# Four operand buffers with tiles 548 instead of 544 elements apart, in a two-layer hybrid encoder step

## What is computed

```python
def trunk(x, ...):
    for i in range(2):
        h = rmsnorm(x, norm_mix[i])
        if i % 2 == 0:
            u, v, z, xbc, dt_raw = split(h @ l0_w_in)
            ya, gm_v = gmlp_mix(u, v, ...)              # spatial gating in chunks of 128
            yb, ... = mamba_mix(z, xbc, dt_raw, ...)    # conv, state-space scan, norm
            x = x + concatenate([ya, yb]) @ l0_w_out
        else:
            x = x + retention_mix(h, ...)               # 8 heads, w_in 1024 x 6144, w_out 2048 x 1024
        h = rmsnorm(x, norm_ffn[i])
        x = x + (silu(causal_dwconv(h @ w_gate)) * (h @ w_up)) @ w_down      # d_ff 2816
        gate = sigmoid(rmsnorm(x, norm_ple[i]) @ ple_w_gate[i])
        x = x + gate * (p[i] @ ple_w_proj[i])
    return rmsnorm(x, norm_final), ...
```

## Time and profile before

| | |
|---|---|
| median of 3 runs | 1999.78 us (1998.51 to 2000.27) |
| span of the profiled execution | 1997.0 us |
| TensorE matmul busy | 1869.7 us, 94% |
| TensorE weight load busy | 1802.0 us, 90% |
| DVE, ACT, POOL busy | 48%, 31%, 44% |
| matmuls | 14,129, of which 12,864 at L310 |
| mean granted TensorE clock | 0.955 of full speed |

### The profile page before, as it was taken

The page is one execution under the profiler, slowest core; times in us unless marked ns, Lnnn a source line. Parts: engine busy times, 40 slices in busy tenths (PEclk is TensorE's granted clock), DMA queues, the critical chain, the costliest instruction groups (busy, mean ns, idle before and its releaser), DMA issues.

```text
span 1997.0 us, 34512 instructions
## 1 busy us (share of the span) xinstructions
PE 1869.7 (94%) x14129; PEld 1802.0 (90%) x14129; DVE 951.5 (48%) x1509; ACT 614.9 (31%) x886; POOL 877.9 (44%) x428
## 2 busy tenths in 40 slices
PE   3996997999999999999989999999989999999996
PEld 2995895789899999999989999999879999999995
DVE  1214585654755255155664444154445534524555
ACT  3241122223432222223443333233323422322342
POOL 4433142323754455456653333333335444544562
PEclk7995696999999999999999999999989999999998
DMA  4230020112123422222322222222212222222221
GB/s 141 85 105 26 23 85 9 43 43 74 64 85 109 135 85 95 96 77 71 106 75 82 82 71 72 94 75 83 72 42 80 93 87 85 95 96 82 71 92 45
DMA packets 49106, 156.23 MB, mean 78 GB/s; under 512 B 5969, under 2 KB 9937, under 8 KB 49010
## 3 DMA queue, kind: packets, MB, share of 16 engines
q1 hardware_dynamic: 43920, 146.75, 22.5%
q10 hardware_dynamic: 5090, 8.13, 1.2%
HBM read 149.23 MB, written 5.63 MB: 78 GB/s over the span
## 4 chain that ended last, share of the span: by engine, by line
PE 83%; DVE 9%; issue 3%; POOL 2%; ACT 2%; DMA 0%; DVEq 0%; SPq 0%; POOLq 0%; ACTq 0%
PE proj L310 73%; PE Q L891 8%; DVE arena L1361 1%; DVE op_lo L380 1%; DVE arena L1582 1%; ACT arena L601 1%; POOL ssq L396 1%; POOL arena L526 1%; DVE arena L1278 1%; PE Q L1111 0%; ACT op_hi L367 0%; DVE rstd L360 0%; POOL w_lo L405 0%; DVE x L1584 0%; DVE arena L1470 0%
## 5 line engine op out<-in xcount | busy, mean ns | idle before, releaser
L405 POOL TENSOR_TENSOR w_lo<-w_raw,w_hi 128x1024 fp32r<-128x1024 f32 (+2 forms) x276 | 654.8, 2373 | 817.3 <-ACT w_hi L331 817.0
L310 PE MATMUL proj<-op_hi,w_hi 128*128 128x256 f32 x4288 | 900.0, 291 | 43.6 <-POOL w_lo L405 20.6
L310 PE MATMUL proj<-op_hi,w_lo 128*128 128x256 f32 x4288 | 890.5, 289 | 0.0
L310 PE MATMUL proj<-op_lo,w_hi 128*128 128x256 f32 x4288 | 883.3, 287 | 0.0
L310 PEld LDWEIGHTS proj<-op_hi,w_hi 128*128 128x128 f32 x4288 | 689.2, 189 | 56.4 <-POOL w_lo L405 20.6
L310 PEld LDWEIGHTS proj<-op_lo,w_hi 128*128 128x128 f32 x4288 | 692.5, 189 | 0.0
L310 PEld LDWEIGHTS proj<-op_hi,w_lo 128*128 128x128 f32 x4288 | 688.0, 189 | 0.0
L331 ACT ACTIVATE w_hi<-w_raw 128x1024 fp32r<-128x1024 f32 (+2 forms) x276 | 284.7, 1032 | 710.1 <-PE proj L310 710.0
L1278 DVE TENSOR_TENSOR arena<-proj,rstd 128x512 f32<-128x512 f32 x153 | 105.6, 690 | 273.6 <-PE proj L310 273.0
L1285 DVE TENSOR_TENSOR x<-proj,x 128x512 f32<-128x512 f32 x72 | 49.8, 691 | 261.4 <-PE proj L310 261.4
L891 PE MATMUL Q<-arena 128*128 128x256 f32 (+9 forms) x604 | 140.4, 374 | 23.8 <-POOL arena L526 17.7
(11 more groups left out here) (149 smaller groups left out, 1003.0 us busy)
## 6 DMA issues: line engine op xcount, KB each, us to landing
w_raw<-in_w_gu SPq DMA_DIRECT2D x88, 512.0 KB, 3.3
w_raw<-in_w_down SPq DMA_DIRECT2D x32, 512.0 KB, 3.3
w_raw<-in_w_heads_a SPq DMA_DIRECT2D x30, 512.0 KB, 3.3
w_raw<-in_w_heads_b SPq DMA_DIRECT2D x18, 512.0 KB, 3.2
w_raw<-in_w_gate SPq DMA_DIRECT2D x16, 512.0 KB, 3.3
w_raw<-in_w_xbc SPq DMA_DIRECT2D x12, 512.0 KB, 3.4
w_raw<-in_w_down SPq DMA_DIRECT2D x16, 384.0 KB, 3.0
w_raw<-in_w_v SPq DMA_DIRECT2D x8, 512.0 KB, 4.9
```

Of the source, the lines that this page charges most:

```text
L310: last = nc.tensor.matmul(proj[:, 2 * g.mod(2) + half, 0:size], w[:, lo:lo + P], o[:, at:at + size], start=(k == 0 and j == 0), stop=(k == ...
L405: nc.gpsimd.tensor_tensor(w_lo[:, c:c + width], w_raw[:, c:c + width], w_hi[:, c:c + width], ALU.subtract).then_inc(w_lo_done, 1)
```

## The change

The pitch of the tiles in the four operand buffers becomes OP = T + 4 = 548 elements, so each buffer grows by 32 elements (128 bytes). The four elements behind each tile are never written or read. All reads and writes of the operand buffers use the new pitch. The arena is cut by 84 elements to make room. x and everything else keeps its pitch of 544. Tiles 6 and 7, which were written and read as one run of 1088 elements for p, become two runs of 544 with a gap between them (`two_ops`).

```diff
+OP = T + 4
@@
-        op_hi = [sb(f"op{i}_hi", KD * T, R) for i in range(2)]
-        op_lo = [sb(f"op{i}_lo", KD * T, R) for i in range(2)]
+        op_hi = [sb(f"op{i}_hi", KD * OP, R) for i in range(2)]
+        op_lo = [sb(f"op{i}_lo", KD * OP, R) for i in range(2)]
...
-        ARENA = 15200
+        ARENA = 15116
...
+        def two_ops(buf):
+            return buf[:, 6 * OP:8 * OP].rearrange("p (a b) -> p a b", a=2)[:, :, 0:T]
+
...
-                            at = (k0 + k) * T + half * HALF
+                            at = (k0 + k) * OP + half * HALF
...
-            nc.scalar.activation(part(op_hi[ops], n, 0, T), src, ACT.Copy, scale=col(gain, n))\
+            nc.scalar.activation(part(op_hi[ops], n, 0, T, OP), src, ACT.Copy, scale=col(gain, n))\
...
-            nc.vector.scalar_tensor_tensor(out=part(op_lo[ops], n, 0, T), in0=src, scalar=col(gain, n),
-                                           in1=part(op_hi[ops], n, 0, T), op0=ALU.mult, op1=ALU.subtract)\
+            nc.vector.scalar_tensor_tensor(out=part(op_lo[ops], n, 0, T, OP), in0=src, scalar=col(gain, n),
+                                           in1=part(op_hi[ops], n, 0, T, OP), op0=ALU.mult, op1=ALU.subtract)\
...
-                        run(op_hi[HID[layer]][:, 6 * T:8 * T], p_raw, ACT.Copy, "p_hi")
+                        run(two_ops(op_hi[HID[layer]]), two(p_raw), ACT.Copy, "p_hi")
...
-                        at = k * T + half * HALF
+                        at = k * OP + half * HALF
...
-                            tt(part(op_lo[HID[layer]], n.div(2), 0, T), h, part(op_hi[HID[layer]], n.div(2), 0, T), sub)\
+                            tt(part(op_lo[HID[layer]], n.div(2), 0, T, OP), h, part(op_hi[HID[layer]], n.div(2), 0, T, OP), sub)\
...
-                        tt(op_lo[HID[layer]][:, 6 * T:8 * T], p_raw, op_hi[HID[layer]][:, 6 * T:8 * T], sub)\
+                        tt(two_ops(op_lo[HID[layer]]), two(p_raw), two_ops(op_hi[HID[layer]]), sub)\
```

More of the change, by code:

```diff
@@ L676, in _ @@
                 act.wait_ge(sem("gm_ya"), 2 * g + 2)
-                run(part(op_hi[1], g, 0, T), ya[:, (g % 2) * T:(g % 2 + 1) * T], ACT.Copy, "gm_hi")
+                run(part(op_hi[1], g, 0, T, OP), ya[:, (g % 2) * T:(g % 2 + 1) * T], ACT.Copy, "gm_hi")
             act.dma_start(s_sample, A["ssm_state"]).then_inc(sem("s_in_loaded"), 16)
@@ L785, in turn5 @@
                             act.wait_ge(sem("r_mix"), (h * 4 + (2 * e + 3)).v)
-                            run(part(op_hi[1], tile + e, 0, T), sq[:, e * T:(e + 1) * T],
+                            run(part(op_hi[1], tile + e, 0, T, OP), sq[:, e * T:(e + 1) * T],
                                 ACT.Copy, "r_mhi")
@@ L849, in gate_up @@
                             act.wait_ge(tile_read, (n + (gu.g0 + 1)).v)
-                            run(part(op_hi[HID[layer]], n.div(2), 0, T), hid[:, q * T:(q + 1) * T], ACT.Copy,
+                            run(part(op_hi[HID[layer]], n.div(2), 0, T, OP), hid[:, q * T:(q + 1) * T], ACT.Copy,
                                 "f_hi")
@@ L1224, in turn5 @@
                     dve.wait_ge(sem("r_mhi"), (h * 2 + (e + 1)).v)
-                    tt(part(op_lo[1], tile + e, 0, T), sq[:, e * T:(e + 1) * T], part(op_hi[1], tile + e, 0, T), sub)\
+                    tt(part(op_lo[1], tile + e, 0, T, OP), sq[:, e * T:(e + 1) * T], part(op_hi[1], tile + e, 0, T, OP), sub)\
                         .then_inc(sem("r_mlo"), 1)
@@ L1323, in ya_low @@
                 dve.wait_ge(sem("gm_hi"), g + 1)
-                tt(part(op_lo[1], g, 0, T), ya[:, (g % 2) * T:(g % 2 + 1) * T], part(op_hi[1], g, 0, T), sub)\
+                tt(part(op_lo[1], g, 0, T, OP), ya[:, (g % 2) * T:(g % 2 + 1) * T], part(op_hi[1], g, 0, T, OP), sub)\
                     .then_inc(sem("gm_lo"), 1)
```

## The result

The kernel before takes 1999.18 us (median of 15 runs, 1997.98 to 2000.45), the changed one 2004.7 us (15 runs, 2002.61 to 2005.77). The ratio is 1.0026, with a 95% interval of 1.0018 to 1.0034: slower by 0.26%, some 5.5 us. The two sets of runs do not overlap, so the difference is real, small as it is.

The account below looks back on a forecast made before the run. The prediction took TensorE's matmul pace, 124.7 ns a matmul on L310, to bound the kernel. Its four parts summed to 0 on a median of 1999.8 us, giving 2000.0 us, with a range of 1982 to 2022 us.

Parts of the forecast that it names:

- the forecast's own case: Whole kernel: time stays the same, within about 0.2% (4 us) of no change; chance 0.64.
- Rival A: Moving reads inside a block take one block more: 64-byte blocks 65 us slower, chance 0.07; 32-byte 21.5 us, 0.12.
- Rival B: Starts equal modulo 128 collide, so the change helps: large 110 us faster, chance 0.05; small 17 us, 0.09.
- What bounds the kernel: TensorE has work for 94% of the span; the matmul line L310 is 73% of the chain of waits.
- Part 1: Copies on ACT, subtractions on DVE: no added instructions; second runs cost at most 0.22 and 0.27 us, on the path 0.
- Part 2: DVE and ACT writes into the operand buffers: 0 from starts off 64-byte boundaries, upper bound 4 us, no gain.
- C: Writes into the operand buffers cost their upper bound, the matmul pace unchanged: 2004 us, counted within the forecast's 0.64.
- Part 3: Matmuls' moving reads from the operand buffers: 9684 come to start off a 64-byte multiple, at 0 cost or gain.
- Part 4: Everything behind the operand buffers moves by 512 bytes, with the same residues modulo 512: 0.
- What would show it: Signs if right: 48 gate-phase pairs in 11.97 us, 0.748 us a tile in gu01, L380's minimum at 783 ns.

Follow-up runs that it names:

- the control: Changed kernel's buffer sizes and arena, but pitch 544 as before, so only what lies behind the buffers moves by 512 bytes; 1999.82 us in one run (before: 1999.15).

## Why the prediction was right or wrong, point by point

The forecast was 2000.0 us, "same". It came out 4.7 us above that, inside the range of 1982 to 2022, and slower by 0.26% where the forecast's own case ended at 0.2%. That the time lies in the range is in part luck: the range was spanned by rivals A and B, neither of which happened, and no term of the sum or rival has the mechanism that did. The effect was small enough to fit.

*What bounds the kernel* held. The only thing that moved was TensorE's pace, and it moved the span one to one (5.4 us of busy time, 5.3 us of span).

*Part 1, instructions: 0.* Right: 34,512 before and after, and the two copies of 1088 elements cost the same in two runs as in one (1099 and 1292 ns). The bounds of 0.22 and 0.27 us for a second run were far too wide.

*Part 2, writes: 0, at most 4 us.* Right at 0. C gives nearly the right time, 2004 us, for a reason that didn't occur: the writes kept their durations and the wait on them became shorter. A time that fits doesn't prove the mechanism.

*Part 3, moving reads: 0.* **This is the term that failed.** It measures +20 and +26 ns a slab of 48 matmuls, 0.47 ns a matmul. Over 12,864 matmuls that is 6.0 us at most, of which 5.3 show. The argument was that "every row in which an address varies gives 0". The rows compared tiles of before alone. They differ in the rhythm by up to 20 ns a tile, which I put down to the stream. All of these tiles have the same distance to their weights modulo 128 bytes, so the rows held the one quantity fixed that the change moves. I also asked only for the address of the moving operand, and set the weights aside since 16 columns of them go at the same pace as 128. That row says that the *amount* of weights doesn't matter; the run in which only the weights were moved, +67 ns a slab, says that their *place* does. The sentence on 16-byte cachelines (the Trainium skill, page "SBUF — State Buffer", section "Door 1: The DMA port swizzle") counted as many lines at either pitch, and by it the sum stayed 0. The measured pace differs among layouts with equal counts of such lines, from 5.947 to 6.080 us a slab, so the rule doesn't price this.

*Part 4, the shift by 512 bytes: 0.* Right, shown by the control.

*Rival A* had the sign, not the mechanism. Tile 0, aligned to 64 bytes, takes 0.76 us and tile 3, 48 bytes off, 0.74. The kernel in which nothing is aligned runs at before's pace. And A's prices of 21.5 and 65 us are 4 and 12 times what was found.

*Rival B* (equal starts collide, the change helps) is refuted for this change: the tiles no longer start alike modulo 128 and are slower. Its idea that the rhythm of 0.74 and 0.75 us holds something to be gained has a grain of truth: half of the phases at +16 bytes take 5.947 us. The others take 6.053, and the kernel as a whole is 3.5 us slower.

*What would show it.* The 11.97 us of the gate phase was the right place to look. But its 0.06 us is only six times the 0.01 us to which a start is read, the 0.32 us over 96 tiles is 32 times that; a longer stretch should have been named.

**What stays open** is the mechanism. Shown: the pace depends on the place of the moving read relative to the weight read, and differs between steps of 16 bytes; it depends on more than the distance modulo 128 (two pitches with equal distances differ, and so do slabs 128 bytes apart); it isn't a sum over matmuls; and one layout can have two paces. That looks like two reads of one engine which fall into a repeating pattern with each other, and the pattern's length, not the single read, sets the pace. This is an interpretation, which no run shows directly. Moving w_lo or the PSUM side alone, or other contents of the weights' ring, wasn't tried.

## What to carry to other kernels

Where TensorE streams without waits, its pace in a long stretch (first start to last start of a hundred tiles) is read to a few hundredths of a per cent; take it for each phase before believing a difference of 0.2%. When an operand of a matmul is to be moved or its pitch changed, don't reason from the moving operand's alignment alone: look where the weights start too. The layouts tried here lay between +1.6% and -0.7% of before's pace. If a layout has to move, try to keep the tiles' distance to the weights: tiles and w_hi moved by 16 bytes together (and w_lo by 48) cost nothing here, while a distance kept modulo 128 under another pitch gave back only about half of the loss.

## What the runs showed of the hardware

- 48 one-pass matmuls (256 and 288 columns) of the same shape at the granted clock of 1.00 took from 5.947 to 6.080 us (123.9 to 126.7 ns each), by the places of operands and weights, all of them multiples of 16 bytes.
- w_hi moved by 16 bytes and w_lo by 48: +67 ns a slab, +12.3 us for the kernel (one run each). The tiles moved by 16 bytes as well: 0.
- Equal addresses, two paces: with all tiles at +16, 5.947 us a slab in gu12 and 6.053 in gu11 of the same execution; with pair 1 at +48, 5.973 in down10 and 6.009 in gu01.
- With tiles and weights at pitches of 548 and 132 elements, slabs take 5.96 or 6.04 us by the distance of tiles and ring slot modulo 256.
- The excess over one column a cycle is still unexplained as a whole: 11.4 ns of 124.7 in before, 10.6 ns at the quickest layout and 13.3 at the slowest. No layout took away more than 0.8 ns of it.
